# Feed-forward up products: 512-column products of the rounded weights, with the two halves of a bank added after PSUM

## The reference

```python
h  = rmsnorm(x, norm_ffn_g)              # 256 x 1024
u  = h @ w_up                            # 1024 x 5632: 2816 gate, 2816 value columns
u  = causal_conv(u, conv_w) + conv_b     # 3 taps over the tokens, each column by itself
x  = x + (silu(gate half) * value half) @ w_down     # 2816 x 1024
```

## Time and profile before

| | |
|---|---|
| median of 3 runs | 1162.57 us (1161.79 to 1163.64) |
| the profiled execution | 1158.68 us, of which the span of the trace is 1156.8 us |
| PE matmul, busy | 1086.6 us, 94% |
| DVE, busy | 563.0 us, 49% |
| ACT, busy | 419.6 us, 36% |
| feed-forward of the first block | about 186 to 382 us of the span |
| slabs of w_up in it | 22, with 48 products each |

### The profile page before, as it was taken

How to read it: one execution, slowest core, us unless ns; L and a number is a source line. 1 busy time by engine, 2 the same in 40 slices (tenths; PEclk the granted TensorE clock), 3 DMA queues, 4 the chain that set the end, 5 groups by cost and what they waited for, 6 DMA issues and landing times.

```text
span 1156.8 us, 16062 instructions
## 1 busy us (share of the span) xinstructions
PE 1086.6 (94%) x6197; PEld 739.8 (64%) x6204; DVE 563.0 (49%) x1054; ACT 419.6 (36%) x750; POOL 89.3 (8%) x114
## 2 busy tenths in 40 slices
PE   8999998999999998898999999989889899999996
PEld 5898977899999787675344443358767644444332
DVE  5754375766666556756222222274684722222224
ACT  5355434545455345733111111143474311111111
POOL 1200000000000011520000000011152000000000
PEclk9999998999999999999999999999989999999997
DMA  8743253546555433339999999944241999999992
GB/s 291 262 146 110 87 190 125 181 152 213 181 174 188 140 118 122 111 121 388 421 420 419 420 420 420 417 150 126 75 152 68 365 393 420 419 419 420 420 420 104
DMA packets 81684, 294.56 MB, mean 255 GB/s; under 512 B 7252, under 2 KB 40386, under 8 KB 56914
## 3 DMA queue, kind: packets, MB, share of 16 engines
q1 hardware_dynamic: 79456, 289.29, 65.2%
q10 hardware_dynamic: 1394, 2.18, 0.5%
q0 software_dynamic: 768, 2.19, 0.5%
HBM read 292.59 MB, written 1.05 MB: 254 GB/s over the span
## 4 chain that ended last, share of the span: by engine, by line
PE 77%; DVE 9%; DMA 5%; ACT 5%; issue 3%; POOL 0%; SPq 0%; ACTq 0%; DVEq 0%
PE bank L2289 17%; PE bank L2298 8%; PE bank L1846 7%; PE bank L1847 7%; PE bank L1848 7%; PE bank L1901 4%; PE bank L1902 4%; PE bank L1903 4%; PE bank L1776 4%; PE bank L2276 3%; DMA raw<-in_w_in 3%; PE bank L2321 3%; PE bank L1935 2%; DMA k_t<-in_w_up 2%; PE bank L1919 2%
## 5 line engine op out<-in xcount | busy, mean ns | idle before, releaser
L1092 DVE TENSOR_TENSOR lo<-raw,hi 128x2048 fp32r<-128x2048 f32 (+3 forms) x79 | 168.4, 2149 | 70.3 <-ACT hi L688 70.0
L688 ACT CAST hi<-raw 128x2048 fp32r<-128x2048 f32 (+3 forms) x79 | 140.1, 1796 | 50.8 <-PE bank L1848 46.9
L1901 PE MATMUL bank<-xs,hi 128*128 128x256 f32 x448 | 128.8, 287 | 7.3 <-DVE lo L1092 3.5
L1321 DVE TENSOR_TENSOR proj<-bank,proj 64x512 f32<-64x512 f32 x32 | 34.6, 1082 | 205.2 <-PE bank L2311 192.8
L1846 PE MATMUL bank<-hi,xs 128*128 128x512 f32 (+2 forms) x312 | 124.2, 398 | 9.8 <-DVE gates L1586 5.5
L1902 PE MATMUL bank<-xs,hi 128*128 128x256 f32 x448 | 127.6, 285 | 0.0
L1903 PE MATMUL bank<-xs,lo 128*128 128x256 f32 x448 | 127.6, 285 | 0.0
L1847 PE MATMUL bank<-hi,xs 128*128 128x512 f32 (+2 forms) x312 | 118.2, 379 | 0.0
L1848 PE MATMUL bank<-lo,xs 128*128 128x512 f32 (+2 forms) x312 | 118.1, 379 | 0.0
L1030 ACT ACTIVATE proj<-bank 64x512 f32<-64x512 f32 x32 | 18.8, 589 | 203.5 <-PE bank L2290 203.5
L1901 PEld LDWEIGHTS bank<-xs,hi 128*128 128x128 f32 x448 | 86.8, 194 | 8.9 <-issue 4.4
(11 more groups left out here) (280 smaller groups left out, 2097.7 us busy)
## 6 DMA issues: line engine op xcount, KB each, us to landing
raw<-in_w_up SPq DMA_DIRECT2D x40, 1024.0 KB, 5.2
raw<-in_w_in SPq DMA_DIRECT2D x28, 1024.0 KB, 5.4
moe_w<-in_w_gate SPq DMA_DIRECT2D x24, 1024.0 KB, 16.0
moe_w<-in_w_up SPq DMA_DIRECT2D x24, 1024.0 KB, 17.5
moe_w<-in_w_down SPq DMA_DIRECT2D x24, 1024.0 KB, 16.2
raw<-in_w_down SPq DMA_DIRECT2D x19, 1024.0 KB, 5.7
raw<-in_w_gate SPq DMA_DIRECT2D x10, 1024.0 KB, 13.0
raw<-in_w_o SPq DMA_DIRECT2D x8, 1024.0 KB, 4.9
```

The costliest lines, as they stand in the source:

```text
L688: nc.scalar.copy(high(n)[:, 0:size], raw[:, n % RING, 0:size]).then_inc(S["hi_done"], 1)
L1092: tt(low(n)[:, 0:size], raw[:, n % RING, 0:size], high(n)[:, 0:size].bitcast(F32), ALU.subtract).then_inc(S["lo_done"], 1)
L1901: mm(dst, wh[:, k, col], x_hi, start=k == 0, stop=False)
```

## The change

`up_slab` takes the place of `feature_slab` for the 22 up slabs. Its w_hi product covers `x_hi` and `x_lo` in one instruction of 512 columns, into a whole bank: the left half gets w_hi * x_hi, the right half w_hi * x_lo. w_lo * x_hi (256 columns) is added to the right half. A slab then fills two banks (0 and 1 for g, 2 and 3 for v) instead of one. After the product ACT copies the right halves into `up[side]` (`logit` or `prob`, buffers of SBUF that are free here), DVE adds the left halves (`up_summed`), and the three taps read `up[side]` instead of the bank. PE waits for `up_summed` of the step before instead of `taps_g` and `taps_v`. Two semaphores of other stages become one (`pool_summed`), with the same waits.

```diff
@@ ACT, ffn_step
                     act.wait_ge(S["slab_used"], count(n + side + 1, jj, 6))
+                    for c in range(2):
+                        nc.scalar.copy(up[side][:, c, :], bank[2 * side + c][:, SEQ:2 * SEQ]).then_inc(S["up_copied"], 1)
+                    act.wait_ge(S["up_summed"], j * 4 + 2 * side + 2)
                     if not first:
                         act.wait_ge(S["act_lo"], j)
                     for c in range(2):
                         at = j * 2 + side * FFC + c
-                        nc.scalar.activation(y[:, side, c, :], bank[side][:, c * SEQ:(c + 1) * SEQ], ACT.Identity,
+                        nc.scalar.activation(y[:, side, c, :], up[side][:, c, :], ACT.Identity,
@@ DVE, ffn_step
+                    for c in range(2):
+                        dve.wait_ge(S["up_copied"], j * 4 + 2 * side + c + 1)
+                        tt(up[side][:, c, :], bank[2 * side + c][:, 0:SEQ], up[side][:, c, :], ALU.add).then_inc(S["up_summed"], 1)
+                    dve.wait_ge(S["up_summed"], j * 4 + 2 * side + 2)
                     dve.wait_ge(S["tap2"], j * 4 + 2 * side + 2)
...
-                                out=dst, in0=bank[side][:, c * SEQ:(c + 1) * SEQ - back],
+                                out=dst, in0=up[side][:, c, 0:SEQ - back],
@@ PE
+            def up_slab(n, side, j=None, ready=None):
+                wait_slab(pe, "lo_done", n, j, 6)
+                wh, wl = (slab_of(t, n, DC)(256) for t in (hi, lo))
+                for c in range(2):
+                    both = bank[2 * side + c]
+                    for k in range(DC):
+                        if ready and c == 0:
+                            ready(k)
+                        col = slice(c * P, (c + 1) * P)
+                        if k:
+                            mm(both[:, SEQ:2 * SEQ], wl[:, k, col], xs[:, k, 0:SEQ], start=False, stop=False)
+                        ins = mm(both[:], wh[:, k, col], xs[:, k, :], start=k == 0, stop=k == DC - 1)
+                        if k == 0:
+                            mm(both[:, SEQ:2 * SEQ], wl[:, k, col], xs[:, k, 0:SEQ], start=False, stop=False)
+                ins.then_inc(S["slab_used"], 1)
...
-                    pe.wait_ge(S["taps_g"], j * 2)
-                    feature_slab(n, DC, 256, [bank[0]], j=jj, per=6)
-                    pe.wait_ge(S["taps_v"], j * 2)
-                    feature_slab(n + 1, DC, 256, [bank[1]], j=jj, per=6)
+                    for side in range(2):
+                        pe.wait_ge(S["up_summed"], j * 4 + 2 * side - 2)
+                        up_slab(n + side, side, jj)
```

More of the change, by code:

```diff
@@ L148 @@
  qk_summed qk_gained rope_products rope_summed
- pairs_turned pairs_copied keys_copied pooled_summed pooled_copied mixed_summed mixed_hi mixed_lo
+ pairs_turned pairs_copied keys_copied pool_summed pooled_copied mixed_hi mixed_lo
  gated ab_summed half_out left_out heads_turned heads_high heads_low x_updated
  scores logits bias_ready probs flipped probs_turned weighted sums_inverted heads_saved
- acc_closed tap2 tap1 taps_g taps_v silu_done act_ready act_hi act_lo
+ acc_closed up_copied up_summed tap2 tap1 taps_g taps_v silu_done act_ready act_hi act_lo
  in_saved0 in_saved1 qup_saved0 qup_saved1 kv_saved0 kv_saved1 pads_zero
@@ L308, in build @@
         act_s = act_r[:].rearrange("p (b c s) -> p b c s", b=2, c=2)
+        up = [logit, prob]
         vu = wide_a[:].rearrange("p (a n) -> p a n", a=HALVES)
@@ L841, in _ @@
             gates_copied(1)
-            w.next("pooled_summed")
+            w.next("pool_summed")
             for i in range(2):
@@ L866, in _ @@
             splits_to(S_BA + 1)
-            w.next("mixed_summed")
+            w.next("pool_summed")
             for g in range(GROUPS):
@@ L1527, in ffn_step @@
                         split_lo(n + 3, jj, 6)
+                    for c in range(2):
+                        dve.wait_ge(S["up_copied"], j * 4 + 2 * side + c + 1)
+                        tt(up[side][:, c, :], bank[2 * side + c][:, 0:SEQ], up[side][:, c, :], ALU.add)                            .then_inc(S["up_summed"], 1)
+                    dve.wait_ge(S["up_summed"], j * 4 + 2 * side + 2)
                     dve.wait_ge(S["tap2"], j * 4 + 2 * side + 2)
@@ L1995, in _ @@
                              start=half == 0, stop=half == HALVES - 1)
-            ins.then_inc(S["pooled_summed"], 1)
+            ins.then_inc(S["pool_summed"], 1)
             feature_slab(S_GATE + 1, DC, 256, [bank[1]])
@@ L2048, in _ @@
                          start=True, stop=True)
-            ins.then_inc(S["mixed_summed"], 1)
+            ins.then_inc(S["pool_summed"], 1)
             feature_slab(S_BA + 1, 4, 512, bank[2:4])
@@ L2069, in down @@
                             apart=int(last))
-            feature_slab(S_FFN, DC, 256, [bank[0]], ready=fm_chunk)
+            def up_slab(n, side, j=None, ready=None):
[13 more added lines that the diff above has]
+                ins.then_inc(S["slab_used"], 1)
+            up_slab(S_FFN, 0, ready=fm_chunk)
             fm_ready()
             open_acc()
-            feature_slab(S_FFN + 1, DC, 256, [bank[1]])
+            up_slab(S_FFN + 1, 1)
             with pe.Fori(0, (N_FF - 1) // 2) as jj:
```

## The result

| | before | changed |
|---|---|---|
| median | 1163.11 us (1161.79 to 1164.21, 4 runs) | 1177.26 us (1172.85 to 1182.04, 4 runs) |
| the profiled execution | 1158.68 us, span 1156.8 | 1172.85 us, span 1171.0 |
| one turn of DVE in steady steps | 16.98 us | 18.09 us |
| g(0)'s first product to the end of the x adds | 195.43 us | 209.86 us |

The ratio is 1.0134, 95% interval 1.0094 to 1.0175: the change costs 14 us, and both profiled executions, 14.2 us apart, tell the same. (The kernel before, run 100 times beside the experiments, has a median of 1162.2 us. One run fell in a slower state, with a mean granted clock of 0.925 and 1176.9 us, and is left out everywhere; the other 99 take from 1156.4 to 1167.4, with the clock from 0.979 down to 0.965.

A forecast was written before the change was run, and what follows sets the result against it. PE set the pace before at 16.98 us a step; after the change DVE's chain with ACT would, at 18.08. Ten turns +13.2 and the chain ahead +0.8 make +14.0: 1162.6 + 14.0 = 1176.6 us, 80% range 1169.5 to 1182.

The forecast's parts named there:

- DVE's turn: One low part of v to the next: 13.69 us without PE waits, 18.08 after the change, above PE's 16.57.
- the adds: Two 256-column adds on DVE per side and step, behind a low part: 0.69 us, between 0.65 and 0.84.
- the handover to ACT: From the second add's end to ACT's first tap: 0.30 us for g, 0.17 for v.
- the first taps: Two taps on ACT per side, during which DVE can do nothing: 1.02 us, formerly under PE work.
- Ten turns: First to last L1544: 10 x 18.08 = 180.8 us instead of 167.62, that is +13.2.
- v(0)'s chain: Ahead of the ten turns: two copies, an add and a handover, 1.1 us, less 0.3 from PE's slabs: +0.8.
- The stage's end: Behind the last L1544: no added time, since DVE's low parts and x adds already set the end.
- The clock: Longer PE waits before v(1) and the last down may drop it; about 1 us uncovered at down, only in the range.
- SBUF in place of a bank: Taps reading `up`: 0.12 us a turn more on ACT and 0.06 on DVE.
- The rival that rested on it: SBUF is the cheaper source for DVE's taps: 17.5 us a turn, +8.2, 1170.8 us; chance 16%.
- What PE saves: One 512-column product for two of 256: 0.0125 us on each of 32 triples a step, 0.4 us.
- The rival "PE stays the bound": DVE's additions stay under 2.9 us a turn, so the kernel gets faster: -3 us, 1159.5; chance 4%.

The follow-up runs named there:

- run 100: No label of a follow-up: the kernel before, unchanged, was executed 100 times beside the experiments; median 1162.2 us, one slow execution left out.
- the run with work in the gap: Changed kernel with only DVE's order altered: low parts of down and of the next g stand behind the adds of g and v; 1166.76 us, ratio 1.0035.
- the runs with v one place on and v(1) earlier: Changed kernel with each v rounded and lowered a step earlier, v(1) between g(0)'s taps and v(0)'s adds; 1163.16 us, again 1164.76 us.

## Why the prediction was right

The median was forecast at 1176.6 us and came at 1177.26; the difference of the profiled executions was forecast as +14.0 and is +14.2. The mechanism is the forecast one too: DVE's and ACT's chain, not the products, bounds the turn, and both taking the answer away and covering it give PE the bound back.

- **DVE's turn**: 18.08 forecast, 18.09 measured in all ten, to 0.01. Its terms: the adds 0.69 net forecast, 0.67 for g and 0.68 for v measured (for v from the low part's end at 251.78 + 2.28 to the adds' end at 254.74); the handover to ACT 0.30 and 0.17 forecast, 0.24 and 0.16 measured; the first taps 1.02 plus 0.06 for SBUF, 1.10 measured; from their end to DVE's start 0.16 forecast, 0.22 and 0.21 measured. The errors of 0.01 to 0.06 us cancel. That the chain, not the busy share, is what DVE has to give was the step that carried the number.
- **Ten turns** +13.2: measured +13.25. That v(1)'s wait would grow to about 4.2 and cost nothing more under DVE's lateness: 4.26, and the first turn is 18.1 as the others.
- **v(0)'s chain** +0.8: from g(0)'s first start to the first act_lo it is 19.48 us instead of 18.99, so +0.5 here. That is one draw: up to there two other runs have the changed kernel's code, and they took 19.60 and 20.20.
- **The stage's end** 0, with up to 1 us for the clock: +0.69. The run with products on zeros ahead of the last `down` shows that all of it is the low clock. The clock was rightly put in the range; it belonged in the sum.
- The rest: g(0) starts 0.56 us sooner in this execution and what follows the stage takes 0.33 more; the change touches neither. 13.25 + 0.49 + 0.69 - 0.56 + 0.33 = 14.2.
- **SBUF in place of a bank**: ACT +34 ns a first tap (forecast 30), DVE +3 ns a tap (forecast 7). The gain on DVE estimated by the page "VectorE: DVE Perf Modes" of the Trainium skill (section on the TRN2 errata), 65 ns a tap, did not appear: 482 against 479 ns. The rival that rested on it fell with that. On ACT the trace agrees in sign and about in size with the estimate by the same table of the Trainium skill, 43 ns.
- **What PE saves**: 0.0125 us a triple was rounded up, since the rows give 0.240 - 0.228 = 0.012. The products alone saved 0.35 us a step, not 0.4; as PE doesn't bound, that changed nothing. Slabs take 5.59 us (5.56 forecast), the steady wait before v 1.13 us by the row (1.5 forecast). From start to start it is 245.59 - 244.07 = 1.52 us where 0.23 is usual, 1.3 more.
- **The rival "PE stays the bound", priced at -3 us**, was priced too well even for a free chain: the products alone, with no copy and no add, shortened the stage by 1.6 us only, with a longer first turn and a longer chain of v(0).

## What to carry to other kernels

An engine with a third of its time idle may have no room at all: take its turn without the waits for the bound engine, and compare that. Work that makes another engine answer costs the answer too, and an in-order list fills it only if independent work is written between the question and the place where the answer is needed (here 10 of 14 us, with no instruction changed). Before speeding up the engine that bounds, look for the one place where it waits: here moving v(1)'s rounding into the first step, and that of every later v one place on with it, gained 4.4 us of the stage with no new instruction, as much as the whole form was to save.

## What had not been expected of the hardware

- The length of PE's wait did not settle what the granted clock did behind it. Before v(1) the clock stayed at 1.00 around a wait of 2.81 us and fell to 0.50 behind waits of 2.98, 3.83, 3.97, 4.09, 4.25 and 4.26 us. But before the last `down` it stayed at 1.00 behind 2.55 us (the run with the first tap on DVE, below first) and fell to 0.50 behind 1.90 us (the run with work in the gap, below second) and behind 2.57 us (the runs with v one place on and v(1) earlier). What decides between them is not shown here.

```profile
381.10 0.50 PE L1850 MATMUL bank<-hi,act_r 128*128 128x512 f32 x1 [2.55 <-DVE act_r L1548]
382.00:384.00 2.00, 2.00 (x11) 1.62 (x10) 1.85 (x1) 1.93 (x2) 0.00 (x0) 1.00 0.00 0
...
376.60 0.78 PE L1854 MATMUL bank<-hi,act_r 128*128 128x512 f32 x1 [1.90 <-DVE act_r L1552]
378.00:380.00 2.00, 2.00 (x6) 1.58 (x5) 2.00 (x2) 1.42 (x1) 0.00 (x0) 0.50 0.00 0
```

- DVE waited 0.15 to 0.27 us for its own result where the next instruction reads it under a semaphore, while ACT started 0.16 to 0.24 us behind the adds: here the handover to oneself was no cheaper than that one to another engine. (About 0.04 us, by the prediction's estimate from the rows around L909, is a plain handover between the two.)
- The unchanged part of the kernel behind the stage took 775 to 785 us from one profiled execution to the next, and the granted clock differs in a few stretches of it. Medians of four runs can't settle a difference of 3 us here.
